# A mixture-of-experts stage: another order of expert steps, earlier branches over the general path, last sums by chunk

## The reference

```python
def _moe(h, w_router_l, bias_l, w_gate_l, w_up_l, w_down_l, w_sh_gate_l, w_sh_up_l, w_sh_down_l):
    ...
    scores = jax.nn.sigmoid((xt @ w_router_l).astype(jnp.float32))
    ...
    sel = lax.top_k(cand, TOP_K)[1]
    wts = jnp.take_along_axis(scores, sel, axis=1)
    wts = wts / jnp.sum(wts, axis=-1, keepdims=True) * ROUTED_SCALE
    ...
    def expert_block(args):
        xe, e = args
        return (jax.nn.silu(xe @ w_gate_l[e]) * (xe @ w_up_l[e])) @ w_down_l[e]
    ...
    shared = (jax.nn.silu(xt @ w_sh_gate_l) * (xt @ w_sh_up_l)) @ w_sh_down_l
    return (routed + shared).reshape(b, l, d)
```

## Time and profile before

| | us |
|---|---|
| median of 3 runs | 2771.13 |
| lowest and highest run | 2769.49, 2804.34 |
| profiled execution | 2770.47 |
| its span in the profile | 2768.7 |

### The profile page before, as it was taken

The page is one execution under the profiler, slowest core; times in us unless marked ns, Lnnn a source line. Parts: engine busy times, 40 slices in busy tenths (PEclk is TensorE's granted clock), DMA queues, the critical chain, the costliest instruction groups (busy, mean ns, idle before and its releaser), DMA issues.

```text
span 2768.7 us, 34398 instructions
## 1 busy us (share of the span) xinstructions
PE 2157.2 (78%) x12180; PEld 1120.5 (40%) x12180; DVE 1529.8 (55%) x3269; ACT 900.3 (33%) x2472; POOL 743.0 (27%) x675
## 2 busy tenths in 40 slices
PE   6886777767568686786877768599978879989887
PEld 3542332222012253253434434377876443333332
DVE  5357848578546548866879755546565432212222
ACT  2226333433333324434555554423221111111111
POOL 1113334334334213334554535111111010000000
PEclk9988878777768887888988889899989889999999
DMA  7687999999999727999999899803102299999994
GB/s 306 239 357 273 419 422 401 421 364 372 421 421 416 278 92 296 351 421 398 421 407 414 358 421 403 355 31 107 62 31 99 88 364 412 420 420 420 420 419 186
DMA packets 122694, 894.60 MB, mean 323 GB/s; under 512 B 16400, under 2 KB 16912, under 8 KB 21776
## 3 DMA queue, kind: packets, MB, share of 16 engines
q0 software_dynamic: 77760, 545.30, 48.4%
q1 hardware_dynamic: 44752, 347.01, 30.8%
HBM read 893.82 MB, written 4.72 MB: 325 GB/s over the span
## 4 chain that ended last, share of the span: by engine, by line
PE 43%; DVE 24%; DMA 22%; ACT 6%; issue 3%; POOL 1%; SPq 0%; DVEq 0%; ACTq 0%; POOLq 0%
PE ps L155 41%; DMA ring<-in_peer_uv,idx_u 15%; DVE ring L1640 6%; ACT arena L125 4%; DMA ring<-in_w_gu 4%; DVE arena L76 4%; DVE arena L1640 2%; PE ps L158 2%; DVE iu L113 2%; DVE arena L109 2%; DMA arena<-in_peer_uv,idx_u 1%; DMA arena<-in_w_gu 1%; DVE ring L76 1%; DVE small L93 1%; DVE arena L89 1%
## 5 line engine op out<-in xcount | busy, mean ns | idle before, releaser
L155 PE MATMUL ps<-ring,arena 64*64 64x512 f32 (+3 forms) x4512 | 835.2, 710 | 310.3 <-ACT arena L125 269.3
L155 PE MATMUL ps<-arena 128*128 128x128 f32 (+8 forms) x3496 | 671.7, 491 | 164.9 <-ACT arena L125 122.1
L1640 DVE CUSTOM_DVE_ANT_0 ring<-ring,h 128x1024 f32<-128x1024 f32 x384 | 481.4, 1254 | 258.3 <-DMA ring<-in_peer_uv,idx_u 225.8
L2926 POOL DMA_INDIRECT ring<-in_peer_uv,idx_u x384 | 427.5, 1113 | 558.4 <-PE ps L155 514.4
L155 PEld LDWEIGHTS ps<-ring,arena 64*64 64x64 f32 (+3 forms) x4512 | 212.6, 148 | 795.2 <-ACT arena L125 526.6
L155 PEld LDWEIGHTS ps<-arena 128*128 128x128 f32 (+4 forms) x3496 | 338.7, 174 | 417.8 <-ACT arena L125 208.7
L125 ACT ACTIVATE arena<-arena 128x1 f32<-128x1 f32 (+1 forms) x1051 | 269.1, 256 | 647.7 <-DVE arena L1640 581.9
L125 ACT ACTIVATE arena<-ps 128x512 f32<-128x512 f32 (+2 forms) x278 | 156.2, 562 | 793.5 <-PE ps L155 708.7
L155 PE MATMUL ps<-ring,hT 128*128 128x512 f32 (+2 forms) x800 | 265.5, 487 | 8.0 <-DVE hT L84 4.4
L76 DVE TENSOR_TENSOR arena<-arena,ps 128x256 f32<-128x256 f32 (+1 forms) x106 | 57.9, 546 | 348.0 <-ACT arena L125 309.2
L1640 DVE CUSTOM_DVE_ANT_0 arena<-arena,h 128x1024 f32<-128x1024 f32 x128 | 159.8, 1249 | 111.1 <-DMA arena<-in_peer_uv,idx_u 101.5
(11 more groups left out here) (129 smaller groups left out, 1662.0 us busy)
## 6 DMA issues: line engine op xcount, KB each, us to landing
ring<-in_w_gu SPq DMA_DIRECT2D x98, 1024.0 KB, 21.8
ring<-in_w_down SPq DMA_DIRECT2D x52, 1024.0 KB, 21.1
ring<-in_peer_wq SPq DMA_DIRECT2D x16, 2048.0 KB, 10.8
arena<-in_w_gu SPq DMA_DIRECT2D x30, 1024.0 KB, 21.3
ring<-in_w_in SPq DMA_DIRECT2D x10, 2048.0 KB, 20.0
ring<-in_w_mod SPq DMA_DIRECT2D x16, 1024.0 KB, 9.3
arena<-in_w_in SPq DMA_DIRECT2D x6, 2048.0 KB, 11.3
ring<-in_w_gates SPq DMA_DIRECT2D x12, 1024.0 KB, 4.9
```

The lines of the kernel that those rows point to most:

```text
L155: return self.e.matmul(o, lhsT, rhs, start=start, stop=stop, skip_group_check=True)
L1640: v.done(v.e.tensor_tensor_reduce(out=row, in0=row, in1=h[:, n // 128, :], scale=1.0, scalar=0.0, op0=ALU.mult, op1=ALU.add, accum_out=aa[ ...
L2926: g.e.indirect_dma_start(out=landing(l, n), out_offset=None, in_=d["peer_uv"], in_offset=bass.IndirectOffsetOnAxis(ap=idx_u[:, n:n + 1], a ...
```

## The change

It does four things.

1. The steps come in another order. `GROUPS` lists three groups: four pairs (ranks 24 to 31), then four times single, pair, quad, then again four times single, pair, quad. `expert_steps` and `group_of` read from it. The one-hot rounds follow: the first group needs one round and covers steps 0 to 3, the second three rounds and steps 4 to 15, the third three rounds and steps 16 to 27. There are seven rounds as before.
2. `advance(more, 3)` instead of 4: now the first round, the first table and the round of the singles of the second group stand ahead of the steps. POOL's fetch of step s waits for its own group's table.
3. In `add`, TensorE waits for both halves of the output and then sums chunk 0 and chunk 1 one after the other. After chunk 0 of the last step it tells `("first sums", 0)`, and ACT's squares of chunk 0 wait for that; those of chunk 1 wait for `("first wave",)`.
4. Each engine goes to the branch over the general path when its own work is done. The wait for `("first wave",)` moves into the `If` branch for DVE, ACT, POOL and SP. ACT waits for `("ffn", "gated")` before its branch.

```diff
+GROUPS = ((0, ((2, 24),)), (4, ((1, 0), (2, 8), (4, 32))), (16, ((1, 4), (2, 16), (4, 48))))
+
+
 def expert_steps():
-    r = []
-    for i in range(8):
-        r += [(8 + 2 * i, 9 + 2 * i), tuple(range(32 + 4 * i, 36 + 4 * i)), (i,)]
-    return r + [(24 + 2 * i, 25 + 2 * i) for i in range(4)]
+    return [tuple(range(rank + by * i, rank + by * i + by)) for _, kinds in GROUPS for i in range(4) for by, rank in kinds]
+
+
+def group_of(s):
+    return max(g for g, (first, _) in enumerate(GROUPS) if s >= first)
...
-SLOTS_AT = ((256, 280, 304), (312,))
+SLOTS_AT = ((256, 264, 288), (312,))
...
                 def slots():
-                    for g in range(3):
-                        by = 3 if g < 2 else 1
+                    chunk = 0
+                    for g, (first, kinds) in enumerate(GROUPS):
+                        by = len(kinds)
                         for k in range(by):
-                            chunk = 3 * g + k
                             places = range(4 * (chunk % 2), 4 * (chunk % 2) + 4)
-                            one_hots(0, chunk, places, range(k, 4 * by, by), STEPS[12 * g + k:12 * g + 4 * by:by],
+                            one_hots(0, chunk, places, range(k, 4 * by, by), STEPS[first + k:first + 4 * by:by],
                                      columns[:, SLOTS_AT[0][g]:])
+                            chunk += 1
                             yield
...
                         pe.wait_ge(*at("spread", wave, s))
                         for o in range(2):
                             pe.wait_ge(*at("out", "down", wave, s, o))
-                            for c in range(2):
+                        for c in range(2):
+                            for o in range(2):
                                 t = pe.mm(tile_of("sums", c, o)[:, :], m.spread[s % 2][:, c * P:(c + 1) * P],
                                           m.yb[s % 2][:, o * 512:o * 512 + 512], False, s == len(steps) - 1)
+                            if c == 0 and s == len(steps) - 1:
+                                pe.done(t, ("first sums", wave))
                         pe.done(t, ("added", wave, s))
...
-                advance(more, 4)
+                advance(more, 3)
...
                 def slots():
-                    for g in range(3):
-                        one_hots(3 * g, 8 + 8 * g, 2)
-                        yield
-                        if g < 2:
-                            one_hots(3 * g + 1, 32 + 16 * g, 4)
+                    chunk = 0
+                    for g, (first, kinds) in enumerate(GROUPS):
+                        for by, rank in kinds:
+                            one_hots(chunk, rank, by)
+                            chunk += 1
                             yield
-                            one_hots(3 * g + 2, 4 * g, 1)
-                            yield
-                        rows(0, g, 12 * g, 12 if g < 2 else 4)
+                        rows(0, g, first, 4 * len(kinds))
                         yield
...
-                advance(more, 4)
+                advance(more, 3)
...
                 experts(0, more)
-                v.wait_ge(*at("first wave"))
+                v.wait_ge(v.sem, v.n)
                 first, seen = v.n, dict(v.seen)
                 with v.e.If(over > 0):
+                    v.wait_ge(*at("first wave"))
                     slots_again()
...
                 experts(0)
-                a.wait_ge(*at("first wave"))
+                a.wait_ge(*at("ffn", "gated"))
+                a.wait_ge(a.sem, a.n)
                 first, seen = a.n, dict(a.seen)
                 with a.e.If(over > 0):
+                    a.wait_ge(*at("first wave"))
                     experts(1)
+                    for c in range(2):
+                        a.wait_ge(*at("ps", "sums", c))
                 with a.e.Else():
                     a.e.sem_inc(a.sem, a.n - first)
-                a.seen = seen
-                a.wait_ge(*at("ffn", "gated"))
+                    a.seen = seen
+                    a.wait_ge(*at("first sums", 0))
                 for c in range(2):
-                    a.wait_ge(*at("ps", "sums", c))
+                    if c:
+                        a.wait_ge(*at("first wave"))
                     for o in range(2):
...
-                        g.wait_ge(*at("slots", wave, 0 if wave else s // 12))
+                        g.wait_ge(*at("slots", wave, 0 if wave else group_of(s)))
...
-                g.wait_ge(*at("first wave"))
                 seen = dict(g.seen)
                 with g.e.If(over > 0):
+                    g.wait_ge(*at("first wave"))
                     experts(1)
...
             sp.wait_ge(*at("over"))
-            sp.wait_ge(*at("first wave"))
             over = sp.e.value_load(flag[0:1, 0:1], min_val=0, max_val=1)
             seen = dict(sp.seen)
             with sp.e.If(over > 0):
+                sp.wait_ge(*at("first wave"))
                 weights(1, lambda n: [])
```

## The result

| | before | changed |
|---|---|---|
| median of 20 runs, us | 2772.08 | 2790.65 |
| lowest, highest | 2768.37, 2804.34 | 2783.20, 2797.39 |
| ratio, changed to before | | 1.0062 (95% interval 1.0052 to 1.0072) |
| profiled execution, its span | 2770.47, 2768.7 | 2789.47, 2787.7 |

The changed kernel is slower by 0.62%, that is 17.2 us (14.4 to 20.0). The forecast was 2781 in a range of 2758 to 2793, so sign, mechanism and range held, and the size was too small by some 7 us.

A forecast was written before the change was run, and what follows sets the result against it. The DMA queue was taken to bound the middle, TensorE the pairs at the end. Last bytes +23.2, bytes to sum -9.5, sum to square -3.7, with rounding +10.1 on 2771.1, gave 2781 us, range 2758 to 2793.

The forecast's parts named there:

- The bound and the ring: Weight queue, at most 13 pieces ahead: piece 44 waits for up(6)'s first half, and everything behind shifts by 23.2 us.
- The end: After the last bytes: sum 8.1 us later instead of 17.6, first square 0.3 us after the sum instead of 4.0.
- the backlog of 17.6 us: Kernel before, at the end: TensorE's last sum comes 17.6 us after the last bytes, because the four pairs are TensorE-bound.
- The early gathers: Step 4's gather, issued after the second table, lands at 2302.5, before turn(4) past 2307: hidden by 5 us.
- The start: Ahead of the expert steps: fewer one-hot rounds, so shared_down begins 1.8 us early (bounds 0 and 4.8).
- The intervals up to up(6): Front steps, up(0) to up(6): each interval taken with its round gives 115.9 us, 2.7 more than before; adds cost 3.2 more.
- The wait of a sum for ScalarE's copy: In every add: starts about 0.63 us later (bounds 0 and 1.0); five lie on TensorE's path up to up(6), 3.2 us.
- The time after piece 44: Weight queue: piece 44 starts 2.5 us after up(6)'s half, at 2371.8, 23.2 us late; last landing 2758.2.
- The sum: Whole run: +23.2, -9.5 and -3.7 us, with rounding +10.1 against the profiled span, forecast 2781.
- Rival 1: Front: the ring does not starve, last bytes at about 2735, a run of 2758; chance 0.16 with its part-way forms.
- Rival 3: End: TensorE still lags at step 27, so the backlog stays; a run of 2791; chance 0.03.
- Rival 2: Front: TensorE slower at a lower clock, 3.4 to 8.5 us more, runs of 2785 to 2790; chance 0.11.

The follow-up runs named there:

- e4: Changed kernel with the last group's three one-hot rounds and table in steps 6 to 9 instead of 3 to 6; ratio to before 1.0040.
- e6: Changed kernel with 11 places for weight pieces instead of 13; ratio to before 1.0082.
- e1: Kernel before with only the new order of steps, groups, rounds and first advance; sums and branches as before; ratio to before 1.0068.
- e3: Changed kernel with the old half-by-half order of sums in all steps but the last; ratio to before 1.0045.
- e7: Kernel before, with its own order of steps and sums; only the branches are early; ratio to before 0.9980.
- e5: Changed kernel with the four small pairs in the middle, first advance of 4, and half-by-half sums except in the last step; ratio to before 0.9960.

## Why the prediction was right, and where its size was off

**The bound and the ring: right.** The forecast said that piece 44 is the last one gated, that it waits for the first half of up(6), and that everything behind it shifts. In the changed kernel that half ended at 2380.3 - 3.5 = 2376.8, piece 44 landed at 2381.8, and the last piece 386.4 us after it. In all kernels of the table except e4, where a later gate took over, the last piece lands 384.8 to 386.6 us after piece 44, though piece 44 itself moves by 37 us. e6 moved the gate by two pieces and shifted the end by about two pieces.

**The end: right, slightly too dear.** From the last bytes to the first square 8.4 us were forecast and 7.3 measured. ScalarE's branch took 2.7 us, not 4.0: I had taken the gap of the earlier trace rows for a price of one branch. (Before, the slowest engine's last landing was 2735.4 and not 2735, so the backlog of 17.6 us in the forecast was 17.2.) That the chunks released one by one would gain nothing was right, since the sums of chunk 0, the first half of the 3.67 us from 2772.88, were finished before the branch was through at 2775.2. No run has a branch of ScalarE under full queues, so what the forecast says of that is not shown.

**The early gathers: right.** The gather of step 4 never held up turn(4): it landed at 2306.1, and turn(4) came at 2318.2. The interval behind up(3) is the one with the singles' round; it took 23.9 us against 23.4 before, and the 0.5 is no more than the wait in the sums.

**The start: mis-sized.** I took 1.8 us off; up(0) ended only 0.6 us earlier after the flag. TensorE's timeline shows where the rest went (the answer to the earlier trace rows):

```profile
2235.68 3.17 PE L155 MATMUL ps<-arena 128*128 128x2 f32 x16 [2.32 <-DVE arena L76]
2238.70 9.23 PE L155 MATMUL ps<-ring,arena 128*128 128x512 f32 x16
```

The same 16 products of the singles took 3.17 us and not 2.38, and shared_down 9.23 and not 8.79, together the missing 1.2 us. The stretches of just these products show why, by the granted clock (third number from the end; 1.00 is 2.4 GHz, and in between the clock was for a part of the stretch at its lower level of 0.50, that is 1.2 GHz). Before:

```profile
2232.30:2234.68 2.38, 2.38 (x16) 2.29 (x16) 0.00 (x0) 0.00 (x0) 0.00 (x0) 0.78 1.04 427
2237.09:2245.88 8.79, 8.79 (x18) 3.90 (x19) 0.00 (x0) 0.00 (x0) 3.90 (x4) 0.81 0.91 357
```

In the changed kernel:

```profile
2235.68:2238.85 3.17, 3.17 (x17) 3.17 (x18) 1.39 (x2) 0.00 (x0) 2.56 (x3) 0.57 1.00 414
2238.70:2247.93 9.23, 9.23 (x19) 4.04 (x20) 0.00 (x0) 0.00 (x0) 1.59 (x2) 0.77 0.77 311
```

Length times clock is the same for both: 1.86 and 1.81, 7.12 and 7.11. The work is the same, and only its share at the lower level differs. Ahead of the singles' products TensorE had been idle for 2.32 us instead of 0.78; whether that is what lowered the clock was not tried by itself.

**The intervals up to up(6): mis-sized by 3.6 us.** The sum was 115.9 + 3.2 = 119.1; measured 122.7. Two terms are in it. The wait of a sum for ScalarE's copy was put at 0.63 us; where no round stands the changed kernel's step is 16.7 us, and 15.9 to 16.0 in e1 and e3, so it is 0.8, and over the five steps the profiles of the changed kernel and e3 differ by 3.9 us. This was inside the bounds given. The rest, 2.9 us, is that a round does not cost the same in another place: in e1 and e3, which have the new order without the wait, the intervals sum to 118.8 and not to 115.9. I had carried each interval over with its round, and with it, unseen, the clock that was granted in it. Before, the second, third and fifth interval (the rounds of quads, singles and pairs):

```profile
2272.90:2291.80 18.90, 16.08 (x114) 7.28 (x114) 5.12 (x11) 2.45 (x6) 0.99 (x1) 1.00 1.01 416
2291.80:2315.30 23.50, 20.67 (x100) 9.71 (x101) 5.12 (x11) 2.53 (x7) 0.99 (x1) 0.85 0.99 405
2331.50:2352.50 21.00, 18.17 (x85) 8.49 (x86) 5.12 (x11) 2.53 (x7) 0.99 (x1) 0.92 1.01 418
```

In the changed kernel, the fifth and sixth (pairs and quads):

```profile
2335.80:2359.10 23.30, 19.92 (x98) 8.65 (x98) 5.12 (x11) 2.53 (x7) 0.99 (x1) 0.85 0.57 198
2359.10:2380.30 21.20, 17.89 (x156) 8.06 (x157) 5.13 (x11) 2.44 (x6) 0.99 (x1) 0.92 0.68 262
```

The sixth was put at 19.0 us, the price of a quads' round at a full clock, and ran at 0.92; the fifth was put at 20.9, the price at 0.92, and ran at 0.85. What the clock takes is, by an estimate from these rows, the length times what is missing to 1.00: 3.5 - 1.7 = 1.8 us more in the fifth and 1.7 more in the sixth, 3.5 in all against the 2.9 to be explained (an upper figure, since in a part of each stretch TensorE waits for other engines). The same happens between two executions of the same code up to there. In e7, which has the rounds in the places of before, the second interval and the third are these:

```profile
2272.40:2294.30 21.90, 19.03 (x114) 8.75 (x114) 5.12 (x11) 2.46 (x7) 0.98 (x1) 0.84 1.01 418
2294.30:2316.10 21.80, 19.02 (x100) 8.48 (x101) 5.12 (x11) 2.50 (x7) 0.98 (x1) 0.92 0.97 391
```

They took 21.9 and 21.8 us at 0.84 and 0.92 where the earlier trace rows has 19.0 and 23.4, at 1.00 and 0.85. So a price read from one execution holds the clock of that execution. A quads' round costs 3.1 us over the 15.9 of a step when the clock stays full.

**The time after piece 44: 2.5 us.** 1.6 us are a slightly slower tail (386.4 against 384.8 us from the landing of piece 44), for which no run shows a reason. The rest is in the two anchors: piece 44 landed 5.0 us after the half of up(6), where the forecast comes to 4.5 (2.5, and the 2.0 from 2348.6 to the landing of piece 44 before, at 2350.6), and the last landing before was 0.4 us later than the 2735 that I read.

**The sum.** Start 1.2, intervals 3.6, after piece 44 2.5, end -1.1: 6.2 us, against the 6.3 between the 16.4 us of the stage and the 10.1 forecast. The whole loss was a difference of two large terms, +23.2 and -13.1 in the forecast, +30.2 (544.2 - 514.0) and -13.9 (7.3 against 21.2 to the first square) in the profiles.

**The rivals.** Rival 1, that the ring does not starve, is out by the stretch at 284 GB/s. Rival 3, that TensorE still lags at the end, is out by the wait that ends at 2768.2. Rival 2, a slower TensorE at the front, was a part of what happened. Its place was right, and its mechanism too: of the 4.8 us by which start and intervals were mis-sized, 0.7 are the longer wait of the sums, and the other 4.1 go with the lower granted clock, by the rows and the estimate above. That is within the 3.4 to 8.5 us that it named. With 2790.65 us the run is just above the 2773 to 2790 that the forecast gave to its own mechanism, and at the top of this rival's; the range of 2758 to 2793 holds because it took the rival in. What lowers the clock was not varied by itself: in e4, without three of the rounds before up(6), the mean clock from up(0) to up(6) is 0.95, against 0.89 in the changed kernel.

## What to carry to other kernels

When a transfer queue runs a fixed number of pieces ahead and is the bound, count which piece is freed by which step before reordering: steps with few bytes and much fixed work belong where the consumer has a lead (here the middle), not at the front, where each microsecond of theirs, up to the last gated piece, arrives at the last landing, and a step whose work is short against its bytes belongs at the end. A reordering of sums that was meant for the end was paid for in every step; if at all, apply it in the last step alone (what it gives there, no run shows by itself). Take a step's price together with the clock that was granted in it: the same 16 products took 2.38 us at 0.78 and 3.17 us at 0.57.

## What the runs showed of the hardware that I had not expected

A taken branch over the general path took ScalarE 3.8 us before, when ScalarE, VectorE and POOL all branched at 2752.6. It took 2.5 us in the changed kernel (2772.8 to 2775.2) and 2.6 us in e7 (2750.6 to 2753.2), where the engines branch at different times, though VectorE's still overlaps it: in the changed kernel VectorE goes from 2771.15 to 2774.28, 3.1 us against 3.8 before. Whether it is the company that makes the difference was not tried by itself.

The 16 DMA engines finished the last piece up to 12 us apart, in the landing records 2723.7 to 2735.4 before and 2756.8 to 2768.2 in the changed kernel. At piece 44 they were 2.0 us apart before and 0.3 us in the changed kernel, whose queue had just run dry. In e1, e3 and e4, whose queues had run dry too, it was 0.3 to 0.6 us, in e5 and e7, whose queues had not, 1.8. So the starved stretch brought them together, and the spread grew back in full by the end. The Trainium skill, "DMA: Bandwidth & Descriptors", section "Latency and other measured facts", says that two of the sixteen are usually slower. The traces here agree as far as they can: of the last piece's sixteen landings the two latest stand apart (2733.5 and 2735.4 after 2731.3 before, 2767.4 and 2768.2 after 2764.7 in the changed kernel), but the landing records do not name the engine. They also show that the spread builds up with time under a full queue.
